# The last 512 columns between stages: PE transposes replaced by a turn in squares, a store and a fetch

## The reference, cut to what matters

```python
def first_block(x, ...):
    h = x
    h = h + 0.5 * swiglu(rmsnorm(h, ffn1_norm), ffn1_w_in, ffn1_w_out)
    u = rmsnorm(h, mix_norm) @ w_in_mix
    ...
    h = h + jnp.concatenate([y_pool, y_gla], axis=-1) @ w_out_mix
    h = h + 0.5 * swiglu(rmsnorm(h, ffn2_norm), ffn2_w_in, ffn2_w_out)
    return rmsnorm(h, final_norm)

def second_block(x, ...):
    for i in range(2):
        # i = 0: sparse attention a; i = 1: stick-breaking attention b,
        # whose keys and values come from x @ w_kv_b
        h = mixer(x, ...)                     # ends in (o * silu(gate)) @ w_o
        x = layer_norm(ALPHA * x + h, ln_g[i], ln_b[i])
        x = x + (p[i] @ w_p[i]) * sigmoid(x @ w_g[i])
    return x
```

## Time and profile before

| | |
|---|---|
| time, median of 3 runs | 2716.78 us |
| profiled execution, its own time | 2716.57 us |
| its span | 2714.9 us |
| PE busy | 2696.3 us, 99% |
| DVE busy | 1565.5 us, 58% |
| ACT busy | 1303.3 us, 48% |
| DMA queue of SP, share of the 16 engines | 63.9% |
| granted TensorE clock | 1.00 |

### The profile page before, as it was taken

The page is one execution under the profiler, slowest core; times in us unless marked ns, Lnnn a source line. Parts: engine busy times, 40 slices in busy tenths (PEclk is TensorE's granted clock), DMA queues, the critical chain, the costliest instruction groups (busy, mean ns, idle before and its releaser), DMA issues.

```text
span 2714.9 us, 34340 instructions
## 1 busy us (share of the span) xinstructions
PE 2696.3 (99%) x12182; PEld 2221.2 (82%) x12182; DVE 1565.5 (58%) x1946; ACT 1303.3 (48%) x1728; POOL 58.0 (2%) x66
## 2 busy tenths in 40 slices
PE   9999999999999999999999999999999999999999
PEld 7888888888888788888888888887888878878877
DVE  6555555555734466555555555658556576566566
ACT  6443444344544445443444344554554464575463
POOL 0000000000000000000000000030000000021000
PEclk9999999999999999999999999999999999999999
DMA  9876677676845477776676666764457566546754
GB/s 308 261 215 194 209 216 217 192 217 193 263 142 165 147 228 216 218 217 200 207 217 217 193 209 202 245 198 155 140 175 252 168 208 229 174 140 207 238 175 137
DMA packets 422136, 550.06 MB, mean 203 GB/s; under 512 B 40976, under 2 KB 267536, under 8 KB 421232
## 3 DMA queue, kind: packets, MB, share of 16 engines
q1 hardware_dynamic: 420352, 539.90, 63.9%
q0 software_dynamic: 1504, 8.34, 0.9%
q10 hardware_dynamic: 144, 0.04, 0.0%
HBM read 525.06 MB, written 23.07 MB: 202 GB/s over the span
## 4 chain that ended last, share of the span: by engine, by line
PE 95%; DVE 2%; POOL 1%; ACT 1%; DMA 1%; issue 0%; SPq 0%; ACTq 0%; DVEq 0%; POOLq 0%
PE bank L1357 30%; PE bank L1359 30%; PE bank L1358 30%; DVE wlo L1699 1%; POOL rope_b L881 1%; DMA raw<-in_ffn_w_in_dram 1%; PE bank L1316 1%; PE bank L1067 0%; PE bank L829 0%; PE bank L813 0%; PE bank L1058 0%; SPq L1235 0%; ACT whi L1442 0%; PE bank L1051 0%; DVE isc L938 0%
## 5 line engine op out<-in xcount | busy, mean ns | idle before, releaser
L1699 DVE TENSOR_TENSOR wlo<-raw,whi 128x1024 fp32r<-128x1024 f32 (+2 forms) x975 | 1149.7, 1186 | 1079.7 <-ACT whi L1442 1074.6
L1442 ACT CAST whi<-raw 128x1024 fp32r<-128x1024 f32 (+2 forms) x975 | 986.0, 1016 | 1283.4 <-PE bank L1359 1273.0
L1357 PE MATMUL bank<-whi,p_hi 128*128 128x512 f32 x2016 | 790.7, 392 | 3.4 <-DVE wlo L1699 3.4
L1359 PE MATMUL bank<-whi,p_lo 128*128 128x512 f32 x2016 | 784.7, 389 | 0.0
L1358 PE MATMUL bank<-wlo,p_hi 128*128 128x512 f32 x2016 | 784.5, 389 | 0.0
L1357 PE MATMUL bank<-whi,q_hi 128*128 128x512 f32 x1696 | 664.7, 392 | 2.7 <-DVE wlo L1699 2.7
L1359 PE MATMUL bank<-whi,q_lo 128*128 128x512 f32 x1696 | 660.3, 389 | 0.0
L1358 PE MATMUL bank<-wlo,q_hi 128*128 128x512 f32 x1696 | 660.1, 389 | 0.0
L1357 PEld LDWEIGHTS bank<-whi,p_hi 128*128 128x128 f32 x2016 | 378.4, 188 | 86.6 <-issue 7.8
L1359 PEld LDWEIGHTS bank<-whi,p_lo 128*128 128x128 f32 x2016 | 378.4, 188 | 79.2
L1358 PEld LDWEIGHTS bank<-wlo,p_hi 128*128 128x128 f32 x2016 | 378.5, 188 | 78.6 <-issue 1.2
(11 more groups left out here) (288 smaller groups left out, 1008.6 us busy)
## 6 DMA issues: line engine op xcount, KB each, us to landing
raw<-in_ffn_w_in_dram SPq DMA_DIRECT2D x704, 256.0 KB, 3.1
raw<-in_ffn_w_out_dram SPq DMA_DIRECT2D x320, 256.0 KB, 3.4
raw<-in_w_in_a_dram SPq DMA_DIRECT2D x192, 256.0 KB, 3.4
raw<-in_w_in_mix_dram SPq DMA_DIRECT2D x128, 256.0 KB, 3.2
raw<-in_w_ple_gate_dram SPq DMA_DIRECT2D x128, 256.0 KB, 3.9
raw<-in_w_in_b_dram SPq DMA_DIRECT2D x128, 256.0 KB, 3.1
raw<-in_w_out_mix_dram SPq DMA_DIRECT2D x64, 256.0 KB, 3.5
raw<-in_w_o_a_dram SPq DMA_DIRECT2D x64, 256.0 KB, 3.9
```

The source lines that it names most:

```text
L1357: pe.matmul(o, xht, wh, start=(kt == t_first), stop=False)
L1359: ins = pe.matmul(o, xlt, wh, start=False, stop=(kt == t_last))
L1442: act.copy(whi[:, c % SPLIT, 0:n, 0:w], raw[:, c, 0:n, 0:w]).then_inc(hi_done, 1)
L1699: dve.tensor_tensor(wlo[:, c % SPLIT, 0:n, 0:w], raw[:, c, 0:n, 0:w], whi[:, c % SPLIT, 0:n, 0:w].bitcast(F32), ALU.subtract).then_inc(lo_ ...
```

## The change

At all six joins block 3 takes the way of blocks 0 to 2. The two batches of PE transposes and their splits go (`nxt.before` is no longer filled). DVE turns block 3 too, right behind its evacuation. SP has the stores behind its loads of chunk 3 of the next stage's round 1 and the fetch behind its loads of chunk 5 of that round (for blocks 0 to 2 it stays chunk 4). ACT and DVE have `block_hi` and `block_lo` of block 3 where the splits of the batches were. The signals between ACT, DVE and PE now come for each half block of two tiles, and PE waits ahead of each of the 8 chunks of round 0 for the half that it needs: ahead of chunk 6 for the first half of block 3, ahead of chunk 7 for the second. The load of the next layer norm's gains into `bc`, which shares its place with the turned blocks, waits for block 3 instead of block 2.

```diff
@@ building the stages
-                turned_blocks += s.n - 1
+                turned_blocks += s.n
                 s.turned, s.turn_from = (ab["turned_b"], ab["moved_b"]), tm
-                nxt.before.setdefault(0, []).extend(Batch(columns(tm), nxt.pair, 4 * (s.n - 1) + 2 * j) for j in range(2))
...
-                nxt.before.setdefault(0, []).extend(
-                    Batch(columns(h), pair, 4 * (s.n - 1) + 2 * j, s.turn_gain) for j in range(2))
@@ SP
                 if s.turn0 + k:
-                    sp.wait_ge(blk_done, s.turn0 + k)
+                    sp.wait_ge(blk_done, 2 * (s.turn0 + k))
...
                             move_block(*block)
+                        if s.after is not None and isinstance(k, int) and k == 1 and c in (3, 5):
+                            (store_block if c == 3 else move_block)(s.after, s.after.n - 1)
@@ POOL
-                pool.wait_ge(blk_done, by_name[("a_gate", "b_gate")[i]].turn0 + 3)
+                pool.wait_ge(blk_done, by_name[("a_gate", "b_gate")[i]].turn0 * 2 + 8)
@@ PE
-                            if s.after is not None and c % 2 == 0 and c < 6:
-                                pe.wait_ge(blk_done, s.after.turn0 + c // 2 + 1)
+                            if s.after is not None:
+                                pe.wait_ge(blk_done, 2 * s.after.turn0 + c + 1)
@@ ACT, block_hi and second_half
-                ins.then_inc(blk_hi, 1)
+                    if j % 2:
+                        ins.then_inc(blk_hi, 1)
...
+                    if s.after is not None and peeled and k == 0:
+                        block_hi(s.after, s.after.n - 1)
@@ DVE, block_lo and the round
-                dve.wait_ge(blk_hi, s.turn0 + k + 1)
                 for j in range(4):
                     kt = 4 * k + j
+                    if j % 2 == 0:
+                        dve.wait_ge(blk_hi, 2 * (s.turn0 + k) + j // 2 + 1)
...
-                ins.then_inc(blk_done, 1)
+                    if j % 2:
+                        ins.then_inc(blk_done, 1)
...
+                    if s.after is not None and peeled and k == 0:
+                        block_lo(s.after, s.after.n - 1)
...
                     evacuate(s, k, u)
-                    if s.turn0 is not None and k < s.n - 1:
+                    if s.turn0 is not None:
                         turn_block(s, k)
```

More of the change, by code:

```diff
@@ L1752, in block_lo @@
                         ins = dve.tensor_tensor(lo_, src, hi_.bitcast(F32), ALU.subtract)
[L1753 to L1756, removed]
-                ins.then_inc(blk_done, 1)
+                    else:
+                        for t in range(TT):
+                            ins = dve.scalar_tensor_tensor(lo_[:, t, :, :], src[:, t, :, :], vec[:, s.turn_gain + kt:s.turn_gain + kt + 1],
+                                                           hi_[:, t, :, :].bitcast(F32), ALU.mult, ALU.subtract)
+                    if j % 2:
+                        ins.then_inc(blk_done, 1)
             def turn_block(s, k):
```

## The result

The changed kernel took 2741.97 us (median of 4 runs, 2738.57 to 2742.65) against 2717.25 us before (median of 4): ratio 1.0089, 95% interval 1.0076 to 1.0101. It is 0.9% slower. The forecast was 2726.7 us with a range to 2733: the direction was right, the size was not. The profiled execution took 2738.57 us with a span of 2736.7 us, 21.8 us longer than the span before.

A forecast was written before the change was run, and what follows sets the result against it. PE was taken to bound the kernel, busy 99% of the span. From 2716.57 us, minus 5.3 for transposes plus 15.2 for waits gave 2726.5, or 2726.7 against the median; range for 8 in 10, 2720.5 to 2733 us.

The forecast's parts named there:

- PE's transposes: Eight transposes on PE at each of six joins, 0.88 us lost per join: removing them wins 5.3 us.
- the sum: Forecast's total over the joins: 5.3 us won from transposes, 15.2 us lost to PE's waits and refills.
- DVE's turn costs nothing but at J5: DVE's 1.31 us turn ahead of chunk 4's split: hidden except at the fifth join, 0.9 us there with refill.
- The place of the waits: PE idles ahead of chunk 6 at all six joins, released by `block_lo`, with 0.6 us ahead of chunk 4 at the fifth.
- Stores to fetch: Block 3's stores to issue of its fetch: 4.3 us at the first three joins, 3.9 us at the others.
- The fetch: Block 3's 512 KB fetch at medians: 4.6 us (first three joins), 5.4 (fourth, sixth), 6.4 (fifth).
- The clock: Rival: TensorE's clock halves after the fifth join's wait, chunks 6 and 7 cost 5.4 us more, 2732.1 us; chance 0.06.
- The slow-fetch rival: Rival: fetches slow beside the weight loads, each taking 6.6 us, giving 2735 us; chance 0.06.
- In-time landing: Rival: block 3's round trip lands in time, stores 3.3 us and fetches 3.2, giving 2716.3 us, not slower; chance 0.12.

The follow-up runs named there:

- E5: E2 with the fifth join (`gate0`) alone going back to the PE transposes of the kernel before: 2712.76 us, ratio 0.9986 to the kernel before.
- E4: Changed kernel without stores and fetch of block 3, its 32-row groups not exchanged, so the last 512 columns are misplaced: 2712.10 us, ratio 0.9984.
- E6: E2 with SP waiting until block 3's fetch has landed before loading chunks 4 to 7 of round 1: 2714.64 us, ratio 0.9992.
- E2: Changed kernel with block 3's fetch right behind its stores, no load of weights between: 2716.36 us, ratio 0.9998 to the kernel before.
- E1: Changed kernel with block 3's fetch behind the load of chunk 4 instead of chunk 5: 2726.92 us, ratio 1.0040 to the kernel before.
- E3: Changed kernel with 53 extra matmuls, results overwritten, filling PE's waits ahead of chunk 6: 2736.11 us, ratio 1.0069 to the kernel before.
- E7: E2 with half-block signals undone, DVE and PE waiting for all four tiles: 2730.17 us, ratio 1.0047 to the kernel before.

## Why the prediction was right in kind and wrong in size

- **PE's transposes, 5.3 us: right.** E5 returns 3.9 us for five joins (4.4 by the sum), E4 4.6 us for six with J5's wait at chunk 4 against it (4.4 by the sum).
- **DVE's turn costs nothing but at J5: right.** 0.64 us idle at J5's chunk 4, as block 2 had shown, and no other wait on `wlo` at a join; E4 confirms it.
- **The place of the waits: right.** All six stand ahead of chunk 6, released by `block_lo`; none at chunk 7.
- **Stores to fetch, 3.9 and 4.3 us: right but for J3.** 4.2 us at J1, 4.3 at J2, 3.8 at J4 to J6; at J3 it was 4.7, as the fetch there stands behind a load that waits for a split which two small operations of DVE delay. The 5.83 us that I had read at J3 stop ahead of these.
- **The fetch: the step that failed.** I took medians of 4.6, 5.4 and 6.4 us "as the same loads of weights run beside the fetch", and wrote one sentence later that two chunks' loads stood ahead instead of one. That was the cause, and I gave it no price. Measured: 3.2 us with nothing around it (E6), 3.2 to 4.1 with loads behind it only (E2), 4.2 to 5.7 with one chunk ahead (E1), 5.9 to 6.6 with two (changed kernel). The waits came to 19.1 us idle and 2.1 of refill, 21.2, where the sum had 15.2; the six fetches took 37.5 us where I had assumed 31.0, which explains the 6 us.
- **The clock: a rival I gave 0.06, and for J5 alone.** It fell behind four of six waits, behind the 1.84 us of J6 too, and cost about 6 us in the profiled execution (6.4 from the windows, 5.8 from E3). The sum put it at nothing. I had reasoned from the longest wait before, 1.4 us, and from J5's 5 us, and left out what lay between. By "TensorE: Matmul & The Clock Gate" of the Trainium skill, section "HAM oscillation — how this bites in real kernels", an idle gap that is long enough puts the array back to half clock; the trace agrees for J3 and J5 (3.78 and 5.02 us). The page's rule allows gaps like those of J2 and J6 (3.08 and 1.84 us), behind which the clock fell here too, and the measurement decides. The slow-fetch rival was right as well, and the two came together, which no case of mine had: 6.0 us for the fetches and about 6 for the clock are the 12 us by which the profiled execution's account exceeds my sum.
- **In-time landing**: the rival of the other side is E2. The mechanism was real, but it needs the fetch in another place. That E2's 2716.36 us meet the rival's 2716.3 is luck: the rival had 0.8 us each at J1 to J3 and 2.4 at J5; E2 has 0.24 us at J3 and nothing at J1 and J2, and at J5 2.6 us idle, two refills and a clock fall.

## What to carry to other kernels

When a transfer is on the critical path, what is issued right ahead of it on the same queue delays it: put it ahead of the prefetches, which have slack, and price it by a transfer with the same number of bytes queued ahead, not by the median of its kind. Even that price is a range: with one chunk ahead of each, the fetches of blocks 0 to 2 took 3.2 to 6.6 us. A new wait on an otherwise full TensorE costs its idle time, 0.3 us of refill, and, from the 1.8 us of J6 on, possibly another 1.6 us of clock. Decide a swap join by join by the slack: with the fetch right behind the stores, the way by DRAM pays here where 9 us or more lie between the end of the turn and the use, and not with 5.8; no join lies between.

## What the runs showed of the hardware that was not expected

- A fetch of 512 KB from DRAM took 3.2 us alone (E6); each chunk of weights (two loads of 256 KB) issued just ahead added 1.3 to 1.4 us on the mean of the six joins (E2, E1, changed kernel), the same loads issued just behind 0 to 0.8 us (E2 against E6).
- The granted clock fell to half behind idle times of 3.08, 3.78, 5.02 and 1.84 us (changed kernel), 2.48 (E1), 1.93 (E2), 2.08 and 3.20 (E7), and did not behind 3.16 (changed kernel), 2.38 (E1), 2.20 and 2.32 us (E7), nor behind any wait of 1.60 us or less at the joins: the length of the idle time alone does not decide it. With some of each wait filled with matmuls (E3) it fell behind none of six, with idle times up to 2.65 us; as it also stayed up behind some unfilled waits of 2.2 to 2.4 us, whether the filling itself kept it up is not shown.
- The clock's level is paid in time even in the kernel before: of its 48 runs beside the experiments, the six with a mean granted clock of 0.999 took 2717.84 to 2720.05 us, the 42 with 1.000 took 2715.82 to 2717.81.
